# Experts of a mixture-of-experts stage taken in blocks of 64 tokens, not 32, and a new order of the half-width products

## The chip, the cores and the metric

The kernel runs on one core of one Trainium2 chip. The metric is device time in microseconds (us) of one execution; the smaller is the better.

## What is computed

Three transformer blocks one after the other on a sequence of 256 tokens, model width 1024, all in 32-bit floats. The change touches the mixture of experts of the first block and some projections of all three. The mixture, cut to what matters:

```python
logits = h @ w_router + b_router            # 256 tokens, 32 experts
top_v, top_i = lax.top_k(logits, 4)         # each token goes to 4 experts
gates = softmax(top_v)
# for each expert e and the tokens xb that chose it:
u = xb @ w_mlp1[e] + b_mlp1[e]              # 1024 -> 2048
x_glu = minimum(u[..., ::2], 7.0)
x_lin = clip(u[..., 1::2], -7.0, 7.0)
a = x_glu * sigmoid(1.702 * x_glu) * (x_lin + 1)
y = a @ w_mlp2[e] + b_mlp2[e]               # 1024 -> 1024
# out[token] += gate * y
```

The weights of an expert are 12 MB, so that the 32 experts read 384 MB.

## The kernel before

**The expert loop.** An expert's tokens are taken in passes of at most `C1` = 32; every expert has at least one pass. VectorE computes on the chip how many passes each expert needs and writes a list to `work`; all engines loop over that list. In one pass TensorE does the following, in the order of `expert_pass`: the first half of the up product of pass n (`up(n, 0, e)`), the transposes of the hidden activations of pass n-1 (`turn_hidden`), the gather of the tokens of pass n+1 by a product with a 0/1 matrix (`gather`), the down product of pass n-1 (`down`), the transposes of the gathered tokens (`turn_tokens`), the second half of the up product with the bias row (`up(n, 1, e)`), the product that adds the outputs of pass n-1 to the four sum banks (`scatter`), and the transposes of the way back (`back`). ScalarE copies each result out of PSUM, VectorE does the gated activation.

**Narrow products.** With 32 tokens as the stationary operand a matmul uses 32 of TensorE's 128 columns. The up product therefore puts four blocks of 512 output columns side by side, each in a strip of 32 columns (`C1 * c`), all in bank 0 of PSUM; gather and down do the same. Each product of 32-bit floats stands in the trace as two matmul instructions, so that the up product has 64 of them in a pass, and the down product 32.

**The slabs.** An expert's weights lie in six slabs of 2 MB, each with one place in SBUF and no second buffer. Slabs 0 to 3 hold `w_mlp1`: 0, 1, 2 in `ring`, 3 in `MOD`. Slabs 4 and 5 hold `w_mlp2`: 4 in `HTY`, 5 in `scr`. Slabs 0 to 3 are loaded by SP's queue, 4 and 5 by POOL's. The load of the next expert into a place is issued when the last pass of the expert before has used it: for 0, 1 and 2 after each one's last matmul, for 3 at the end of the up product, for 4 at the middle of `down` (`down_begun`) and for 5 at its end (`down`):

```python
pool.wait_ge(m1["down_begun"], through)
expert_slab(e, 4)
pool.wait_ge(m1["down"], through)
expert_slab(e, 5)
```

**The half-width products.** `features` computes a projection with features on the partitions. Where an argument is a pair (`twice`), the 64 columns of the weights are multiplied twice, into partitions 0 to 63 and 64 to 127 of the bank. The loop (line 702) goes over the eight parts of the contraction, and in it over the two halves; the matmul is on line 704. All other products of this kind go through `mm_k` (line 669).

Of the kernel before, what the change touches and what calls it, by code (L numbers as in the profile page):

```python
# [29 lines left out]
FLOOR = -1.0e20  # L30
C1 = 32
STRIPS1 = 4
PASSES = E1 + TOP1 * S // C1
# [109 lines left out]
def build(nc, I, out, rel_scratch):  # L143
    first, end, first_slab, release = product_plan()
    landed = landed_plan()
    with ExitStack() as ctx:
# [46 lines left out]
        def carve(base, *shape):  # L193
# [42 lines left out]
            "counted", "listed", "masked", "pick", "pick_back", "gather", "slots_read", "turn_tokens", "gather_read", "back", "back_read",  # L236
            "up", "up_read", "glu", "sig", "hidden", "turn", "turn_read", "gates_turned", "gates_read", "down_begun", "down", "down_read",
            "scatter", "sum", "sum_read", "step")}
        m1_slab_used = [sem(f"m1_slab_used{j}") for j in range(3)]
# [35 lines left out]
        b1row = scr[:, 0:BANK]  # L275
        XG, XS, GPT = carve(512, KT, C1), carve(768, S), carve(1024, S)
        PICK, PICKG = carve(1280, NT, C1), carve(1344, NT, STRIPS1, C1)
        glu, lin1, sig, aS = carve(1600, S), carve(1856, S), carve(2112, S), carve(2368, S)
        aT, YS = carve(2624, 2, P), carve(2880, BANK)
        GT, EPLACE, MASK = carve(5248, NT, E1), carve(5312, NT, E1), carve(5376, NT, E1)  # L280
        MASKED, LX = carve(5440, 3 * E1), carve(5536, NT, E1)
        LOGITS1, CHOSEN1, TOPL = carve(5600, NT, 4 + E1), carve(5672, NT, 4 + E1), carve(5744, NT, 8)
        rcur, gcur = carve(5760, NT), carve(5762, NT)
        EPASS, ESTEPS, EMORE = carve(5764, E1), carve(5796, S // C1), carve(3392, E1, S // C1)
        OFFSET1, START1, PASSED1 = carve(3648, PASSES + 2), carve(3714, PASSES + 2), carve(7084, PASSES + 2, E1)
        WORK = carve(3780, END1)
        gatesT = scr[0:E1, 5804:6060]
        b2row = scr[0:E1, 6060:7084]

# [257 lines left out]
        def _(pool):  # L547
# [77 lines left out]
            with pool.Fori(1, E1) as e:  # L625
                through = pool.value_load(work[0:1, bass.ds(e + (THROUGH - 1), 1)], min_val=1, max_val=PASSES)
                pool.wait_ge(m1["down_begun"], through)
                expert_slab(e, 4)
                pool.wait_ge(m1["down"], through)
                expert_slab(e, 5)  # L630

# [18 lines left out]
        def _(pe):  # L650
# [45 lines left out]
            def features(cols_of, rhs=HT, nk=KT, m=P):  # L696

                b = bank()
                for i, c in enumerate(cols_of):
                    if isinstance(c, tuple):  # L700

                        for k in range(nk):
                            for half in range(2):
                                mm = pe.matmul(b[64 * half:64 * half + 64, S * i:S * (i + 1)], c[half](k), rhs[:, k, :],  # L704
                                               start=k == 0, stop=k == nk - 1)
                    else:
                        mm = mm_k(b[0:m, S * i:S * (i + 1)], c, lambda k: rhs[:, k, :], nk)
                close(mm)
# [240 lines left out]
            def gather(n):  # L949

                pe.wait_ge(m1["pick"], n + 1)
                if not (isinstance(n, int) and n == 0):
                    pe.wait_ge(m1["gather_read"], n)
                for a in range(NT):
                    for q in range(STRIPS1):
                        mm = pe.matmul(ps[C1 * q:C1 * (q + 1), 3, 0:S], PICK[:, a, :], H[:, a, S * q:S * (q + 1)],  # L956
                                       start=a == 0, stop=a == NT - 1)
                mm.then_inc(m1["gather"], 1)

            def turn_tokens(n):  # L960

                pe.wait_ge(m1["slots_read"], n + 1)
                for i in range(2):
                    mm = pe.transpose(ps[:, 3, P * i:P * (i + 1)], XS[:, i:S:2], ident[:, :])
                mm.then_inc(m1["turn_tokens"], 1)
# [9 lines left out]
            def up(n, b, e):  # L975
# [3 lines left out]
                for j in (2 * b, 2 * b + 1):  # L979
                    if j == 3:  # L980
                        pe.wait_ge(m1_row_landed, 16 * e + 16)
                    pe.wait_ge(m1_landed[j], 16 * e + 16)
                    for i in range(2):
                        for c in range(STRIPS1):
                            mm = pe.matmul(ps[C1 * c:C1 * (c + 1), 0, :], XG[:, 2 * j + i, :],  # L985
                                           m1_slabs[j][:, i, BANK * c:BANK * (c + 1)], start=j + i == 0, stop=False)
                    if j < 3:
                        mm.then_inc(m1_slab_used[j], 1)
                if b == 1:
                    for c in range(STRIPS1):  # L990
                        mm = pe.matmul(ps[C1 * c:C1 * (c + 1), 0, :], ones[32 * c:32 * c + 1, 0:C1], b1row[32 * c:32 * c + 1, :],  # L991
                                       start=False, stop=True)
                    mm.then_inc(m1["up"], 1)

            def turn_hidden(n):

                pe.wait_ge(m1["hidden"], n + 1)
                pe.wait_ge(m1["back_read"], n + 1)
                for i in range(2):
                    mm = pe.transpose(ps[:, 2, P * i:P * (i + 1)], aS[:, i:S:2], ident[:, :])  # L1000
                mm.then_inc(m1["turn"], 1)

            def down(n, e):

                pe.wait_ge(m1["turn_read"], n + 1)
                for j in (4, 5):
                    pe.wait_ge(m1_landed[j], 16 * e + 16)
                    for i in range(2):
                        for t in range(2):
                            c = 2 * (j - 4) + t  # L1010
                            for half in range(2):
                                r = 2 * C1 * half + C1 * t
                                mm = pe.matmul(ps[r:r + C1, 1, :], aT[:, i, C1 * c:C1 * (c + 1)],  # L1013
                                               m1_slabs[j][:, 2 * t + i, BANK * half:BANK * (half + 1)],
                                               start=j + i == 4, stop=j + i == 6)
                    mm.then_inc(m1["down_begun" if j == 4 else "down"], 1)

            def scatter(n, last=False):

                pe.wait_ge(m1["down_read"], n + 1)  # L1020
                for a in range(NT):
                    for half in range(2):
                        r = slice(2 * C1 * half, 2 * C1 * (half + 1))
                        mm = pe.matmul(sum_bank(a, half), GPT[r, P * a:P * (a + 1)], YS[r, :], start=False, stop=last,  # L1024
                                       skip_group_check=True)
# [5 lines left out]
            def expert_pass(n, e, e_before):  # L1031

                pe.wait_ge(m1["gather_read"], n + 1)
                up(n, 0, e)
                turn_hidden(n - 1)
                gather(n + 1)
                down(n - 1, e_before)
                turn_tokens(n + 1)
                up(n, 1, e)
# [16 lines left out]
            with pe.Fori(1, n_passes) as n:  # L1056
                expert_pass(n, expert_of(n), expert_of(n - 1))
            turn_hidden(n_passes - 1)
            down(n_passes - 1, expert_of(n_passes - 1))
# [286 lines left out]
        def _(act):  # L1346
# [168 lines left out]
            def slots(n):  # L1515
                act.wait_ge(m1["gather"], n + 1)
                act.activation(XS, ps[:, 3, 0:S], ACT.Copy).then_inc(m1["slots_read"], 1)

            def gathered(n):

                if not (isinstance(n, int) and n == 0):
                    act.wait_ge(m1["up"], n)
                act.wait_ge(m1["turn_tokens"], n + 1)
                act.activation(XG.rearrange("p (q i) c -> p i q c", i=2), ps[:, 3, 0:S].rearrange("p (i q c) -> p i q c", i=2, q=STRIPS1),
                               ACT.Copy).then_inc(m1["gather_read"], 1)
# [8 lines left out]

            def turned_hidden(n):
                act.wait_ge(m1["turn"], n + 1)
                act.activation(aT, two(ps[:, 2, :], P), ACT.Copy).then_inc(m1["turn_read"], 1)

            def outputs(n):

                act.wait_ge(m1["scatter"], n + 1)
                act.wait_ge(m1["down"], n + 1)
                act.activation(YS, ps[:, 1, :], ACT.Copy).then_inc(m1["down_read"], 1)  # L1543

            def expert_pass(n):
                turned_hidden(n - 1)
                slots(n + 1)
                outputs(n - 1)
                gathered(n + 1)
# [13 lines left out]
            with act.Fori(1, n_passes) as n:  # L1563
                expert_pass(n)
            turned_hidden(n_passes - 1)
            outputs(n_passes - 1)
# [152 lines left out]
        def _(dve):  # L1719
# [353 lines left out]
            def pick_back(n):  # L2073

                shape = [P, NT, STRIPS1, C1]
                tell(dve.tensor_tensor(PICKG[:, :, :, :], PICK.unsqueeze(2).to_broadcast(shape),
# [37 lines left out]
            def activation(n, astep):  # L2114

                dve.wait_ge(m1["up"], n + 1)
                tell(dve.tensor_scalar(glu, ps[:, 0, 0:BANK:2], 7.0, None, ALU.min), m1["glu"], n + 1)  # L2117
                tell(dve.tensor_scalar(lin1, ps[:, 0, 1:BANK:2], 7.0, -7.0, ALU.min, ALU.max), m1["up_read"], n + 1)
                dve.wait_ge(m1["sig"], n + 1)
# [313 lines left out]
```

## Time and profile before

| | |
|---|---|
| median of 3 runs | 2653.49 us (2651.34 to 2654.19) |
| the profiled execution | 2654.19 us |
| its span in the trace | 2652.4 us |
| busy: TensorE matmuls, VectorE, ScalarE | 2120.5, 500.4, 392.1 us |
| the expert loop of the first block in the trace | 329.19 to 1384.91 us |
| the chain that ended last | PE 61%, DMA 27%, DVE 6%, ACT 3% |

The profiled execution is longer than its span by 1.8 us, which lie around the instructions. PE is TensorE, DVE VectorE, ACT ScalarE, POOL GpSimd, SP the engine that only issues transfers. Busy time says little here by itself: a matmul's time in the trace runs from its start to its modelled end, and neighbours overlap. The distance from one start to the next is what a step costs.

### The profile page before, as it was taken

How to read it: one execution, taken by the hardware profiler on the slowest of the kernel's cores; microseconds unless marked ns; L12 is line 12 of the kernel's file. 1: busy time of each engine (PE TensorE's matmuls, PEld its weight loads, DVE VectorE, ACT ScalarE, POOL GpSimd, SP SyncE). 2: the span in 40 equal slices, each digit the busy share in tenths (PEclk: the TensorE clock that was granted, in tenths of full speed). 3: DMA queues.
4: the chain of work that ended last, by engine and by line, in shares of the span. 5: the costliest groups of instructions: out<-in, count | busy, mean ns of one | idle time of the engine just before them, and what ended most of it. 6: DMA issues, size and time to landing. Idle time of an engine off the chain costs nothing.

```text
span 2652.4 us, 34466 instructions
## 1 busy us (share of the span) xinstructions
PE 2120.5 (80%) x14230; PEld 1185.3 (45%) x14231; DVE 500.4 (19%) x1153; ACT 392.1 (15%) x864; POOL 87.4 (3%) x130
## 2 busy tenths in 40 slices
PE   4976769567767966979779886899969898977785
PEld 3856422112212211322227766689955546453443
DVE  1044421001101100111120375200041302230002
ACT  1142101001101100111111333100001113110011
POOL 4000000000000000000000000000000000000000
PEclk9995779779888987989899995999979999978898
DMA  9460589999999699997952581346424243079964
GB/s 304 121 244 13 208 364 396 426 425 386 384 425 383 284 426 426 373 399 300 384 199 106 197 291 53 127 159 158 136 103 143 104 134 127 32 299 393 391 261 191
DMA packets 170904, 681.33 MB, mean 257 GB/s; under 512 B 15906, under 2 KB 57123, under 8 KB 125520
## 3 DMA queue, kind: packets, MB, share of 16 engines
q1 hardware_dynamic: 149488, 535.79, 52.0%
q0 software_dynamic: 21328, 144.45, 14.1%
q8 instruction: 58, 0.95, 0.1%
q14 instruction: 14, 0.11, 0.0%
q10 hardware_dynamic: 16, 0.02, 0.0%
HBM read 679.17 MB, written 1.06 MB: 256 GB/s over the span
## 4 chain that ended last, share of the span: by engine, by line
PE 61%; DMA 27%; DVE 6%; ACT 3%; issue 2%; SPq 1%; POOLq 0%; DVEq 0%; POOL 0%; ACTq 0%
PE ps L669 29%; DMA scr<-in_w_mlp 20%; PE ps L985 7%; PE ps L1013 6%; DMA MOD<-in_w 5%; PE ps L1284 3%; PE ps L1024 2%; PE ps L746 2%; DMA ring<-in_w_ada 1%; PE ps L704 1%; PE ps L848 1%; PE ps L756 1%; PE ps L956 1%; DVE stat L1749 1%; PE ps L991 1%
## 5 line engine op out<-in xcount | busy, mean ns | idle before, releaser
L985 PE MATMUL ps<-ring,scr 128*32 128x512 f32 x2208 | 289.2, 656 | 65.7 <-DMA ring<-in_w_mlp 63.4
L669 PE MATMUL ps<-ring,HTY 128*128 128x512 f32 (+5 forms) x960 | 331.0, 506 | 3.7 <-ACT HTY L1365 3.7
L669 PE MATMUL ps<-HTY,ring 128*128 128x256 f32 x1136 | 253.1, 386 | 2.4 <-ACT HTY L1365 2.4
L1013 PE MATMUL ps<-scr 128*32 128x512 f32 x736 | 119.9, 782 | 166.9 <-DMA scr<-in_w_mlp 166.9
L669 PEld LDWEIGHTS ps<-ring,HTY 128*128 128x128 f32 x960 | 176.5, 192 | 155.1 <-issue 138.8
L669 PEld LDWEIGHTS ps<-HTY,ring 128*128 128x128 f32 x1136 | 218.2, 193 | 36.1 <-ACT HTY L1365 3.7
L2117 DVE TENSOR_SCALAR scr<-ps 128x256 f32<-128x256 f32 x46 | 19.6, 425 | 822.6 <-PE ps L991 822.5
L985 PEld LDWEIGHTS ps<-ring,scr 128*32 128x32 f32 x2208 | 64.3, 117 | 215.6 <-issue 131.0
L1365 ACT ACTIVATE scr<-ps 128x512 f32<-128x512 f32 (+8 forms) x120 | 59.1, 494 | 527.4 <-PE ps L669 416.5
L1013 PEld LDWEIGHTS ps<-scr 128*32 128x32 f32 x736 | 25.1, 129 | 241.8 <-DMA scr<-in_w_mlp 185.8
L669 PE MATMUL ps<-ring,scr 128*128 128x128 f32 (+1 forms) x1040 | 121.6, 280 | 1.4 <-DVE scr L2221 1.4
L669 PEld LDWEIGHTS ps<-ring,scr 128*128 128x128 f32 x1040 | 117.5, 192 | 5.2 <-issue 3.3
L1284 PE MATMUL ps<-ring,scr 128*32 128x512 f32 x432 | 76.7, 693 | 50.9 <-DMA MOD<-in_w 50.3
L1013 PE MATMUL ps<-HTY,scr 128*32 128x512 f32 x736 | 89.1, 602 | 6.7 <-DMA HTY<-in_w_mlp 6.2
L1024 PE MATMUL ps<-scr 64*128 64x512 f32 x368 | 91.4, 615 | 0.8 <-ACT scr L1543 0.8
L985 PE MATMUL ps<-MOD,scr 128*32 128x512 f32 x736 | 87.3, 592 | 1.0 <-DMA MOD<-in_w_mlp 1.0
L1543 ACT ACTIVATE scr<-ps 128x512 f32<-128x512 f32 x46 | 27.5, 597 | 354.8 <-PE ps L1013 354.8
L669 PE MATMUL ps<-scr,H 128*128 128x128 f32 x320 | 77.9, 405 | 1.6 <-DVE scr L2335 1.6
L746 PE MATMUL ps<-ring,cols 128*32 128x128 f32 x1536 | 51.3, 290 | 34.3 <-DMA ring<-in_w_ada 34.3
L669 PEld LDWEIGHTS ps<-scr,H 128*128 128x128 f32 x320 | 77.0, 335 | 1.7 <-DVE scr L2335 1.7
L1284 PE MATMUL ps<-MOD,scr 128*32 128x512 f32 x144 | 76.6, 693 | 0.0
L1284 PEld LDWEIGHTS ps<-ring,scr 128*32 128x32 f32 x432 | 21.1, 126 | 105.0 <-issue 104.1
(416 smaller groups left out, 2039.5 us busy)
## 6 DMA issues: line engine op xcount, KB each, us to landing
ring<-in_w_mlp SPq DMA_DIRECT2D x96, 2048.0 KB, 14.3
scr<-in_w_mlp POOLq DMA_DIRECT2D x32, 2048.0 KB, 23.9
MOD<-in_w_mlp SPq DMA_DIRECT2D x32, 2048.0 KB, 19.0
HTY<-in_w_mlp POOLq DMA_DIRECT2D x32, 2048.0 KB, 18.9
ring<-in_w_ada SPq DMA_DIRECT2D x24, 2048.0 KB, 9.1
ring<-in_w SPq DMA_DIRECT2D x48, 1024.0 KB, 10.4
ring<-in_w_in SPq DMA_DIRECT2D x21, 2048.0 KB, 7.8
ring<-in_w_ff SPq DMA_DIRECT2D x16, 2048.0 KB, 8.8
```

What stands on the lines that cost most here:

```text
L669: mm = pe.matmul(o, lhs(k), rhs(k), start=begin and k == 0, stop=end and k == nk - 1)
L704: mm = pe.matmul(b[64 * half:64 * half + 64, S * i:S * (i + 1)], c[half](k), rhs[:, k, :], start=k == 0, stop=k == nk - 1)
L746: pe.matmul(b[32 * t:32 * (t + 1), 0:P], csil[:, j, k:k + 1].to_broadcast([P, 32]), w[:, k, P * t:P * (t + 1)], start=k == 0, stop=False)
L756: mm = pe.matmul(b[:, P * t:P * (t + 1)], ident[:, 32 * t:32 * t + 1].to_broadcast([P, P]), ada_quarters[j], start=True, stop=True)
L848: mm = pe.matmul(o, KDb[:, i % 2, pair, P * tile:P * (tile + 1)], QD[:, pair, i, :, :], start=True, stop=True)
L956: mm = pe.matmul(ps[C1 * q:C1 * (q + 1), 3, 0:S], PICK[:, a, :], H[:, a, S * q:S * (q + 1)], start=a == 0, stop=a == NT - 1)
L985: mm = pe.matmul(ps[C1 * c:C1 * (c + 1), 0, :], XG[:, 2 * j + i, :], m1_slabs[j][:, i, BANK * c:BANK * (c + 1)], start=j + i == 0, stop=False)
L1013: mm = pe.matmul(ps[r:r + C1, 1, :], aT[:, i, C1 * c:C1 * (c + 1)], m1_slabs[j][:, 2 * t + i, BANK * half:BANK * (half + 1)], start=j + i ...
L1024: mm = pe.matmul(sum_bank(a, half), GPT[r, P * a:P * (a + 1)], YS[r, :], start=False, stop=last, skip_group_check=True)
L1284: mm = pe.matmul(ps[32 * t:32 * (t + 1), 0, :].rearrange("p (x f) -> p x f", x=2), XG3[:, k, C3 * t:C3 * (t + 1)], m3_slabs[t][:, :, k, :] ...
L1365: act.activation(dst, src, func, **kw).then_inc(product_free, 1)
L1543: act.activation(YS, ps[:, 1, :], ACT.Copy).then_inc(m1["down_read"], 1)
```

## The change

1. `C1` becomes 64. A pass takes up to 64 tokens, and each narrow matmul is 64 columns wide, so that two lie side by side and not four. The up product goes into banks 0 and 1, the gather fills a whole bank, `turn_tokens` has four transposes, the hidden activations are twice as wide and are transposed in two steps through the same half of bank 2 (`turn_hidden(n, 0)`, `turn_hidden(n, 1)`, with a copy by ScalarE between them), and `down` accumulates all four parts of the contraction in bank 2.
2. In the pass, the order is up 0, turn 0, gather, turn 1, `turn_tokens`, down, up 1, scatter, back.
3. POOL issues slabs 4 and 5 together, after `down`.
4. In `features` the halves are the outer loop, the parts of the contraction the inner one.

```diff
-C1 = 32
-STRIPS1 = 4
+C1 = 64
...
-                pool.wait_ge(m1["down_begun"], through)
-                expert_slab(e, 4)
                 pool.wait_ge(m1["down"], through)
-                expert_slab(e, 5)
+                for j in (4, 5):
+                    expert_slab(e, j)
...
-                        for k in range(nk):
-                            for half in range(2):
-                                mm = pe.matmul(b[64 * half:64 * half + 64, S * i:S * (i + 1)], c[half](k), rhs[:, k, :],
-                                               start=k == 0, stop=k == nk - 1)
+                        for half in range(2):
+                            mm = mm_k(b[64 * half:64 * half + 64, S * i:S * (i + 1)], c[half], lambda k: rhs[:, k, :], nk)
...
-                    for q in range(STRIPS1):
-                        mm = pe.matmul(ps[C1 * q:C1 * (q + 1), 3, 0:S], PICK[:, a, :], H[:, a, S * q:S * (q + 1)],
+                    for half in range(2):
+                        mm = pe.matmul(ps[C1 * half:C1 * (half + 1), 3, :], PICK[:, a, :], H[:, a, BANK * half:BANK * (half + 1)],
                                        start=a == 0, stop=a == NT - 1)
...
-                        for c in range(STRIPS1):
-                            mm = pe.matmul(ps[C1 * c:C1 * (c + 1), 0, :], XG[:, 2 * j + i, :],
+                        for c in range(4):
+                            mm = pe.matmul(ps[C1 * (c % 2):C1 * (c % 2 + 1), c // 2, :], XG[:, 2 * j + i, :],
                                            m1_slabs[j][:, i, BANK * c:BANK * (c + 1)], start=j + i == 0, stop=False)
...
-            def turn_hidden(n):
+            def turn_hidden(n, b):
 
                 pe.wait_ge(m1["hidden"], n + 1)
-                pe.wait_ge(m1["back_read"], n + 1)
+                if b == 0:
+                    pe.wait_ge(m1["back_read"], n + 1)
+                else:
+                    pe.wait_ge(m1_turn_read[0], n + 1)
                 for i in range(2):
-                    mm = pe.transpose(ps[:, 2, P * i:P * (i + 1)], aS[:, i:S:2], ident[:, :])
-                mm.then_inc(m1["turn"], 1)
+                    mm = pe.transpose(ps[:, 2, P * i:P * (i + 1)], aS[:, b, i:S:2], ident[:, :])
+                mm.then_inc(m1_turn[b], 1)
 
             def down(n, e):
-
-                pe.wait_ge(m1["turn_read"], n + 1)
+                pe.wait_ge(m1_turn_read[1], n + 1)
                 for j in (4, 5):
                     pe.wait_ge(m1_landed[j], 16 * e + 16)
-                    for i in range(2):
-                        for t in range(2):
-                            c = 2 * (j - 4) + t
-                            for half in range(2):
-                                r = 2 * C1 * half + C1 * t
-                                mm = pe.matmul(ps[r:r + C1, 1, :], aT[:, i, C1 * c:C1 * (c + 1)],
-                                               m1_slabs[j][:, 2 * t + i, BANK * half:BANK * (half + 1)],
-                                               start=j + i == 4, stop=j + i == 6)
-                    mm.then_inc(m1["down_begun" if j == 4 else "down"], 1)
+                    for t in range(2):
+                        for i in range(2):
+                            for s in range(2):
+                                mm = pe.matmul(ps[C1 * s:C1 * (s + 1), 2, :], aT[:, 2 * (j - 4) + i, C1 * t:C1 * (t + 1)],
+                                               m1_slabs[j][:, 2 * t + i, BANK * s:BANK * (s + 1)],
+                                               start=j + t + i == 4, stop=j + t + i == 7)
+                mm.then_inc(m1["down"], 1)
...
                 up(n, 0, e)
-                turn_hidden(n - 1)
+                turn_hidden(n - 1, 0)
                 gather(n + 1)
+                turn_hidden(n - 1, 1)
+                turn_tokens(n + 1)
                 down(n - 1, e_before)
-                turn_tokens(n + 1)
                 up(n, 1, e)
```

ScalarE's and VectorE's instructions in the loop follow the new shapes: their copies and activations read 512 columns where they read 256, and ScalarE has one copy more in a pass.

## Rows read from the trace of the kernel before

**Rows 1.** Timeline of TensorE, one pass that waits for nothing: start, time.

```profile
430.92 3.64 PE L985 MATMUL ps<-ring,scr 128*32 128x512 f32 x32
434.49 0.51 PE L1000 MATMUL ps<-ident,scr 128*128 128x128 f32 x2
434.93 1.07 PE L956 MATMUL ps<-H,scr 128*32 128x256 f32 x16
435.82 1.90 PE L1013 MATMUL ps<-HTY,scr 128*32 128x512 f32 x16
...
439.37 0.50 PE L964 MATMUL ps<-ident,scr 128*128 128x128 f32 x2
...
443.37 1.06 PE L991 MATMUL ps<-scr,ones 1*32 1x512 f32 x8
444.36 1.99 PE L1024 MATMUL ps<-scr 64*128 64x512 f32 x8
...
446.65 0.64 PE L985 MATMUL ps<-ring,scr 128*32 128x512 f32 x4
```

**Rows 2.** Timeline of TensorE, where passes wait for slabs: idle time before, and releaser.

```profile
530.64 1.92 PE L985 MATMUL ps<-ring,scr 128*32 128x512 f32 x16 [2.59 <-DMA ring<-in_w_mlp]
...
971.14 3.64 PE L1013 MATMUL ps<-scr 128*32 128x512 f32 x16 [10.55 <-DMA scr<-in_w_mlp]
...
999.85 3.64 PE L1013 MATMUL ps<-scr 128*32 128x512 f32 x16 [8.93 <-DMA scr<-in_w_mlp]
```

**Rows 3.** Windows, four experts of one pass: busy (x), then clock, DMA share, GB/s.

```profile
484.20:603.90 119.70, 77.81 (x540) 20.58 (x544) 11.00 (x32) 10.21 (x24) 5.64 (x8) 0.80 1.01 426
```

**Rows 4.** The chain that ended last, its first and last piece of line 704.

```profile
79.78 7.06 PE ps L704 x64
...
2208.79 5.33 PE ps L704 x48
```

**Rows 5.** The page's costliest groups: VectorE's first step on an up product.

```profile
L2117 DVE TENSOR_SCALAR scr<-ps 128x256 f32<-128x256 f32 x46 | 19.6, 425 | 822.6 <-PE ps L991 822.5
```

**Rows 6.** Issues of SP's queue in the loop: start, time, line, tile.

```profile
834.53 0.33 SPq L450 DMA_DIRECT2D MOD<-in_w_mlp  x1
...
900.23 0.33 SPq L450 DMA_DIRECT2D MOD<-in_w_mlp  x1
```

**Rows 7.** TensorE's groups by form: busy, mean ns of one, idle before.

```profile
L669 PE MATMUL ps<-HTY,ring 128*128 128x256 f32 x1120 | 249.5, 386 | 2.4 <-ACT HTY L1365 2.4
...
L704 PE MATMUL ps<-HTY,ring 128*64 128x256 f32 x256 | 28.5, 381 | 0.0
...
L704 PE MATMUL ps<-scr,ring 128*64 128x256 f32 x96 | 10.8, 381 | 0.0
...
L669 PE MATMUL ps<-HTY,ring 128*16 128x256 f32 x16 | 3.6, 380 | 0.0
```

**Rows 8.** DMA queues in that window: packets, MB, share of 16 engines.

```profile
q1 hardware_dynamic: 2321, 33.34, 65.7%
q0 software_dynamic: 2294, 17.61, 35.2%
```

**Rows 9.** Timeline of POOL there: an issue of slab 5.

```profile
975.47 0.70 POOL L612 DMA_DIRECT2D scr<-in_w_mlp  x1 [13.36 <-PE ps L1013]
```

**Rows 10.** The page's transfers: how many, KB each, median us from issue to landing.

```profile
ring<-in_w_in SPq DMA_DIRECT2D x21, 2048.0 KB, 7.8
```

**Rows 11.** Timeline of TensorE, the loop's start.

```profile
329.19 8.10 PE L985 MATMUL ps<-ring,scr 128*32 128x512 f32 x48 [0.47 <-ACT scr L1524]
...
338.93 1.06 PE L991 MATMUL ps<-scr,ones 1*32 1x512 f32 x8
...
355.16 5.35 PE L985 MATMUL ps<-ring,scr 128*32 128x512 f32 x32 [1.78 <-issue]
```

**Rows 12.** Timeline of all engines, the loop's end.

```profile
1373.52 1.06 PE L991 MATMUL ps<-scr,ones 1*32 1x512 f32 x8
...
1384.91 1.94 ACT L1569 ACTIVATE HTY<-ps 128x1024 f32<-128x1024 f32 x2 [2.09 <-PE ps L1024]
```

More of the change, by code:

```diff
@@ L236, in build @@
             "counted", "listed", "masked", "pick", "pick_back", "gather", "slots_read", "turn_tokens", "gather_read", "back", "back_read",
-            "up", "up_read", "glu", "sig", "hidden", "turn", "turn_read", "gates_turned", "gates_read", "down_begun", "down", "down_read",
-            "scatter", "sum", "sum_read", "step")}
+            "up", "up_read", "glu", "sig", "hidden", "gates_turned", "gates_read", "down", "down_read", "scatter", "sum", "sum_read", "step")}
+        m1_turn, m1_turn_read = ([sem(f"m1_{n}{b}") for b in range(2)] for n in ("turn", "turn_read"))
         m1_slab_used = [sem(f"m1_slab_used{j}") for j in range(3)]
@@ L275, in build @@
         b1row = scr[:, 0:BANK]
[L276 to L279, printed above, removed]
+        XG, XS, GPT = carve(512, KT, C1), carve(1024, BANK), carve(1536, S)
+        PICK, PICKG = carve(1792, NT, C1), carve(1920, NT, 2, C1)
+        glu, lin1, sig, aS = carve(2176, 2, 256), carve(2688, 2, 256), carve(3200, 2, 256), carve(3712, 2, 256)
+        aT, YS = carve(4224, 4, P), carve(4736, BANK)
         GT, EPLACE, MASK = carve(5248, NT, E1), carve(5312, NT, E1), carve(5376, NT, E1)
@@ L283, in build @@
         rcur, gcur = carve(5760, NT), carve(5762, NT)
[L284 to L288, printed above, removed]
+        EPASS, ESTEPS, EMORE = carve(5764, E1), carve(5796, S // C1), carve(7264, E1, S // C1)
+        OFFSET1, START1, PASSED1 = carve(5800, PASSES + 2), carve(5850, PASSES + 2), carve(7392, PASSES + 2, E1)
+        WORK = carve(5900, END1)
+        gatesT = scr[0:E1, 5984:6240]
+        b2row = scr[0:E1, 6240:7264]
         m1_slabs = [shaped(ring[:, j, :], (2, 2 * F1)) for j in range(3)] + [
@@ L962, in turn_tokens @@
                 pe.wait_ge(m1["slots_read"], n + 1)
-                for i in range(2):
-                    mm = pe.transpose(ps[:, 3, P * i:P * (i + 1)], XS[:, i:S:2], ident[:, :])
+                for jj in range(2):
+                    for i in range(2):
+                        k = 2 * jj + i
+                        mm = pe.transpose(ps[:, 3, P * k:P * (k + 1)], XS[:, S * jj + i:S * (jj + 1):2], ident[:, :])
                 mm.then_inc(m1["turn_tokens"], 1)
@@ L989, in up @@
                 if b == 1:
-                    for c in range(STRIPS1):
-                        mm = pe.matmul(ps[C1 * c:C1 * (c + 1), 0, :], ones[32 * c:32 * c + 1, 0:C1], b1row[32 * c:32 * c + 1, :],
-                                       start=False, stop=True)
+                    for c in range(4):
+                        mm = pe.matmul(ps[C1 * (c % 2):C1 * (c % 2 + 1), c // 2, :], ones[32 * c:32 * c + 1, 0:C1],
+                                       b1row[32 * c:32 * c + 1, :], start=False, stop=True)
@@ L1003, in down @@
             def down(n, e):
-                pe.wait_ge(m1["turn_read"], n + 1)
+                pe.wait_ge(m1_turn_read[1], n + 1)
                 for j in (4, 5):
                     pe.wait_ge(m1_landed[j], 16 * e + 16)
-                    for i in range(2):
-                        for t in range(2):
-                            c = 2 * (j - 4) + t
-                            for half in range(2):
-                                r = 2 * C1 * half + C1 * t
-                                mm = pe.matmul(ps[r:r + C1, 1, :], aT[:, i, C1 * c:C1 * (c + 1)],
-                                               m1_slabs[j][:, 2 * t + i, BANK * half:BANK * (half + 1)],
-                                               start=j + i == 4, stop=j + i == 6)
-                    mm.then_inc(m1["down_begun" if j == 4 else "down"], 1)
+                    for t in range(2):
+                        for i in range(2):
+                            for s in range(2):
+                                mm = pe.matmul(ps[C1 * s:C1 * (s + 1), 2, :], aT[:, 2 * (j - 4) + i, C1 * t:C1 * (t + 1)],
+                                               m1_slabs[j][:, 2 * t + i, BANK * s:BANK * (s + 1)],
+                                               start=j + t + i == 4, stop=j + t + i == 7)
@@ L1022, in scatter @@
                     for half in range(2):
-                        r = slice(2 * C1 * half, 2 * C1 * (half + 1))
+                        r = slice(C1 * half, C1 * (half + 1))
                         mm = pe.matmul(sum_bank(a, half), GPT[r, P * a:P * (a + 1)], YS[r, :], start=False, stop=last,
@@ L1057, in _ @@
                 expert_pass(n, expert_of(n), expert_of(n - 1))
-            turn_hidden(n_passes - 1)
+            turn_hidden(n_passes - 1, 0)
+            turn_hidden(n_passes - 1, 1)
             down(n_passes - 1, expert_of(n_passes - 1))
@@ L1516, in slots @@
                 act.wait_ge(m1["gather"], n + 1)
-                act.activation(XS, ps[:, 3, 0:S], ACT.Copy).then_inc(m1["slots_read"], 1)
+                act.activation(XS, ps[:, 3, :], ACT.Copy).then_inc(m1["slots_read"], 1)
             def gathered(n):
@@ L1523, in gathered @@
                 act.wait_ge(m1["turn_tokens"], n + 1)
-                act.activation(XG.rearrange("p (q i) c -> p i q c", i=2), ps[:, 3, 0:S].rearrange("p (i q c) -> p i q c", i=2, q=STRIPS1),
+                act.activation(XG.rearrange("p (h k) c -> p k h c", h=2), ps[:, 3, :].rearrange("p (k h c) -> p k h c", k=4, h=2),
                                ACT.Copy).then_inc(m1["gather_read"], 1)
@@ L1533, in gate, with turned_hidden @@
                 act.activation(sig, glu, ACT.Sigmoid, scale=1.702).then_inc(m1["sig"], 1)
-            def turned_hidden(n):
-                act.wait_ge(m1["turn"], n + 1)
-                act.activation(aT, two(ps[:, 2, :], P), ACT.Copy).then_inc(m1["turn_read"], 1)
+            def turned_hidden(n, b):
+                act.wait_ge(m1_turn[b], n + 1)
+                act.activation(aT[:, 2 * b:2 * b + 2, :], two(ps[:, 2, :], P), ACT.Copy).then_inc(m1_turn_read[b], 1)
             def outputs(n):
@@ L1542, in outputs @@
                 act.wait_ge(m1["down"], n + 1)
-                act.activation(YS, ps[:, 1, :], ACT.Copy).then_inc(m1["down_read"], 1)
+                act.activation(YS, ps[:, 2, :], ACT.Copy).then_inc(m1["down_read"], 1)
             def expert_pass(n):
-                turned_hidden(n - 1)
+                turned_hidden(n - 1, 0)
                 slots(n + 1)
+                turned_hidden(n - 1, 1)
                 outputs(n - 1)
@@ L1564, in _ @@
                 expert_pass(n)
-            turned_hidden(n_passes - 1)
+            turned_hidden(n_passes - 1, 0)
+            turned_hidden(n_passes - 1, 1)
             outputs(n_passes - 1)
@@ L2073, in pick_back @@
             def pick_back(n):
-                shape = [P, NT, STRIPS1, C1]
+                shape = [P, NT, 2, C1]
                 tell(dve.tensor_tensor(PICKG[:, :, :, :], PICK.unsqueeze(2).to_broadcast(shape),
@@ L2116, in activation @@
                 dve.wait_ge(m1["up"], n + 1)
-                tell(dve.tensor_scalar(glu, ps[:, 0, 0:BANK:2], 7.0, None, ALU.min), m1["glu"], n + 1)
-                tell(dve.tensor_scalar(lin1, ps[:, 0, 1:BANK:2], 7.0, -7.0, ALU.min, ALU.max), m1["up_read"], n + 1)
+                tell(dve.tensor_scalar(glu, ps[:, 0:2, 0:BANK:2], 7.0, None, ALU.min), m1["glu"], n + 1)
+                tell(dve.tensor_scalar(lin1, ps[:, 0:2, 1:BANK:2], 7.0, -7.0, ALU.min, ALU.max), m1["up_read"], n + 1)
                 dve.wait_ge(m1["sig"], n + 1)
```

## Prediction

> **What bounds the kernel now.** I read the chain of waits first. Its pieces in the expert loop are of two kinds: transfers of expert weights, and TensorE's own work. The timeline of TensorE shows that they take turns. An expert that needs several passes gives passes without a wait: the next begins 446.65 - 430.92 = 15.73 us later [rows 1]. An expert of one pass waits for its slabs, for slab 5 above all, and the next pass comes 28.7 us later [rows 2]. There the DMA engines are full: 24 slabs in 119.7 us, 426 GB/s at a share of 1.01 [rows 3], so 4.99 us a slab and 29.9 us an expert. Outside the loop the chain holds long pieces of TensorE work, and all six pieces of line 704 are in it [rows 4].
>
> **How many passes go.** VectorE's first step on an up product ran 46 times [rows 5], so there are 46 passes. An expert of k passes shows as a gap in SP's issues: slab 3 was issued at 834.53 and next at 900.23 [rows 6], 65.7 us later, one waiting pass and two of 15.73. Read in this way, three experts (17, 27 and 31, counted from 0) have three passes, eight have two, 21 have one. Three passes of 32 are 65 to 96 tokens, which are two passes of 64; all others fit in one. So 35 passes stay and 11 go. The bytes stay.
>
> **What a pass costs then.** Four matmuls of 32 columns side by side take as long as one: 32 of 512 columns took 434.49 - 430.92 = 3.57 us [rows 1], which is 8 groups of 0.4275 and 0.15 for the switch of shape. The trace has 64-column matmuls too: 256 of 256 columns on line 704 in 28.5 us, 0.111 each, while full-width ones took 0.223 [rows 7]; two go side by side. So each narrow product needs twice the groups. By steps, from [rows 1]:
> - up, each half: 16 groups, 6.84 + 0.15 = 7.0 (was 3.57).
> - down: 7.0 (was 439.37 - 435.82 = 3.55).
> - gather: 4 groups of 512 columns, 1.8 (was 0.89).
> - transposes of hidden: 0.43 twice. The second waits for a copy, which the gather hides.
> - transposes of tokens: four, 0.8, and about 0.35 before them, since the copy of the gathered bank (some 0.6 to 0.8 us with its start, an estimate from VectorE's 0.425 for half the columns [rows 5]) is covered by 0.43 of transposes only. Behind this wait stands `down`.
> - bias row: four row strips, two column strips, 0.99 if all four run together as now, 1.85 if only two. I take 0.99.
> - scatter and back: unchanged, 446.65 - 444.36 = 2.3. They cover VectorE's two reads of the wider up result (some 0.7 each, twice the columns of [rows 5]) and ScalarE's copy of the next tokens; uncovered, these would cost 1.4.
>
> Sum: 14.0 + 7.0 + 1.8 + 0.86 + 1.15 + 0.99 + 2.3 = 28.1 us, 29.0 with the slower bias. A pass costs 12.4 us more of TensorE's time than one of 32, and comes just under the 29.9 us that an expert's weights take.
>
> **What an expert of one pass costs.** It can't be under 29.9, the slabs, for long. Above that, POOL's queue decides. With both queues at work POOL moved 17.61 MB while SP moved 33.34, in packets equal in number [rows 8], so SP has a slab in 7.5 us and POOL one in 15.0 (16 and 8 of them in 119.7). Slab 5's landings are 999.85 - 971.14 = 28.7 us apart [rows 2], two POOL slabs, 14.2 each when SP pauses, and 975.47 - 971.14 = 4.3 us of it go by while slab 5 is used and issued [rows 2, 9]; slab 4's load fills that gap today. After the change POOL's queue has nothing while slab 5 is used, and both are issued at the end of `down`. Count from there: POOL's data start at 3.4 us (7.8 from issue to landing of a slab [rows 10], less 5.0 of data, plus 0.7 to issue), run alone until SP's slab 2, freed at 3.4, begins at 6.3, and then share. Slab 4 has 2.9/5.0 of itself by then and lands at 12.3 to 12.6, slab 5 at 26.5 to 27.6 (14.2 or 15.0 each), its use takes 3.5: a cycle of 30.0 to 31.1. Were POOL always to share, it would be 3.4 + 30.0 + 3.5 = 37. I take 30.5, the middle. The wait is then 2.4 us a pass; after one of 2.59 us the next 16 matmuls took 1.92 us, after one of 8.93 they took 3.64, at the lower clock [rows 2].
>
> The Trainium skill ("DMA: Bandwidth & Descriptors", Queues, rings and completion order) says each engine goes round the queues packet by packet, so POOL's share would stay a third in pairs too. The equal packet counts agree; by it the even share of a rival below is out.
>
> **The loop's sum.** The first up product took 338.93 - 329.19 = 9.74 [rows 11]; 16 groups more make 16.6, to 345.8. From there to pass 1, 16.2 now [rows 11], 16.5 then. Pass 1 to its bias row: 7.0 + 3.8 + 7.0 + 7.0, to 387.1. Then 33 passes: 28 wait for slab 5 (30.5 each, 854.0), 5 don't, those after the slabs of an expert with two passes (28.1, 140.5). To 1381.6. From the last bias row to the end it was 1384.91 - 1373.52 = 11.4 [rows 12]; `down` adds 3.5, the second turn 1.1: 16.0. End 1397.6, against 1384.9: **+12.7 us.** The 11 passes that go are 11 x 15.73 = 173 us; the 35 left cost TensorE 35 x 12.4 = 434 more, and only what fills the waits of now is free.
>
> **The half-width products.** Halves outside means that neighbours use the same 64 columns. The nearest row is 16 matmuls of 16 columns, one after the other on the same columns: 3.6 us, 0.225 each, as long as full width [rows 7]. So 352 matmuls cost 0.223 and not 0.111: 352 x 0.1115 = **+39.2 us**. All of it is on the chain (six pieces, 38.9 us in sum, [rows 4]), between TensorE work that waits for nothing, idle 0.0 before them [rows 7]; the weights of the next slabs are loaded when TensorE frees a place, so they come later as well. If neighbours overlapped still, it would be 0.
>
> VectorE's tables of the pass list shrink (from 66 rows of 32 to 50); TensorE doesn't wait for them: 0.
>
> Total: 2654.2 + 12.7 + 39.2 = **2706 us**, 1.9% over its own execution; the median of the runs is 0.7 us lower, which the range swallows.
>
> **Rivals.**
> - *TensorE becomes the only bound of the loop* (faster). If slabs came in time always, 33 passes at 28.1 are 927 us, 67 less: 2639. Place: the wait at slab 5. It breaks even with the 39.2 where the 28 passes average 30.5 - 51.9/28 = 28.6 us. Against it: 29.9 of data. For it: the passes of now are 28.7 apart [rows 2]. Chance 0.05.
> - *POOL's pair is late* (much slower): the sharing cycle of 37 in half of the passes, or longer waits that bring the lower clock: 33 on the mean, 28 x 2.5 = 70 more, 2776. Chance 0.12.
> - *The order of halves costs nothing*, TensorE overlapping them otherwise: 2667. Against it [rows 7], chance 0.04.
> - *POOL gets an even share in its pair*: 29.9 a pass, 2689; inside my range, and its chance is in the forecast's.
>
> **How the numbers follow.** Forecast 0.79 (2675 to 2740), rivals 0.05, 0.12, 0.04. A measurement here tells 0.2%, 5 us, from no change. Faster takes the first rival; same is its edge with that of the third: 0.06, 0.04, slower 0.90. The low end, 2668, is the free halves, or 29.1 a pass; the high end, 2755, is 32.3 a pass. Outside lie the first rival and most of the second.
>
> **What would show it.** 35 steps on line 2117's successor, each of 0.69 us; the up half 7.0 us long; passes 30 to 31 us apart with a wait of 2 to 3 us before slab 5's matmuls; DMA share near 1 in them; 28.1 without a wait; line 704 gone, its 352 matmuls in pieces twice as long, 0.22 apart. Wrong if narrow matmuls of two banks don't pair, if POOL's share changes, or if the pieces of the halves stay as short.

## The result, and the profile after

The changed kernel took 2681.84 us (median of 4 runs, 2680.85 to 2687.45) beside 2653.84 us for the kernel before on the same chip: 1.011 times as long, 95% interval 1.0094 to 1.0129. The forecast was 2706 us, range 2668 to 2755.

Its span is 2680.8 us, 28.4 more. The first up product starts at 333.62 instead of 329.19, the loop ends at 1396.33 instead of 1384.91 [rows 11, 12]. So 4.4 us arise before the loop, 7.0 in it (1062.7 for 1055.7), and 17.0 behind it. The two ends of the loop in the timeline of the changed kernel:

```profile
333.62 12.02 PE L983 MATMUL ps<-ring,scr 128*64 128x512 f32 x48 [0.69 <-ACT scr L1524]
...
1396.33 1.94 ACT L1571 ACTIVATE HTY<-ps 128x1024 f32<-128x1024 f32 x2 [2.09 <-PE ps L1022]
```

Such parts scatter by some 4 us from one execution to another: in two of the experiments below, whose kernels are equal up to there, the first up product starts at 331.70 (e1) and 327.60 (e3).

The page of the changed kernel, from its costliest groups (busy, mean ns of one, idle before), with the successor of [rows 5]:

```profile
L2119 DVE TENSOR_SCALAR scr<-ps 128x512 f32<-128x512 f32 x35 | 24.2, 692 | 842.9 <-PE ps L989 842.9
```

There are 35 passes, and VectorE's wider step takes 0.692 us. Next the timeline of TensorE in the changed kernel, a pass that waits for no slab, to be laid beside [rows 1]:

```profile
886.63 0.51 PE L1001 MATMUL ps<-ident,scr 128*128 128x128 f32 x2
887.07 1.94 PE L952 MATMUL ps<-H,scr 128*64 128x512 f32 x8
888.94 0.50 PE L1001 MATMUL ps<-ident,scr 128*128 128x128 f32 x2
889.70 0.75 PE L962 MATMUL ps<-ident,scr 128*128 128x128 f32 x4 [0.26 <-ACT scr L1517]
890.38 3.65 PE L1011 MATMUL ps<-HTY,scr 128*64 128x512 f32 x16
893.87 3.60 PE L1011 MATMUL ps<-scr 128*64 128x512 f32 x16
897.30 3.60 PE L983 MATMUL ps<-ring,scr 128*64 128x512 f32 x16
...
904.27 1.09 PE L989 MATMUL ps<-scr,ones 1*64 1x512 f32 x8
905.28 1.99 PE L1022 MATMUL ps<-scr 64*128 64x512 f32 x8
907.20 0.44 PE L969 MATMUL ps<-ident,scr 128*128 128x128 f32 x2
```

Read from start to start: gather 1.87, transposes of tokens 0.68 after a wait of 0.26 for ScalarE's copy, down 897.30 - 890.38 = 6.92, half of up 904.27 - 897.30 = 6.97, bias row 1.01 (all four of its matmuls side by side), scatter 1.92. The whole pass is 27.96 us.

The same view where a pass waits:

```profile
499.76 5.35 PE L1011 MATMUL ps<-scr 128*64 128x512 f32 x16 [2.57 <-DMA scr<-in_w_mlp]
...
511.91 1.09 PE L989 MATMUL ps<-scr,ones 1*64 1x512 f32 x8
...
530.54 3.65 PE L1011 MATMUL ps<-scr 128*64 128x512 f32 x16 [0.91 <-DMA scr<-in_w_mlp]
...
540.99 1.09 PE L989 MATMUL ps<-scr,ones 1*64 1x512 f32 x8
```

The only slab that passes wait for is slab 5. Among experts of one pass, most passes alternate: one waits 0.7 to 1.0 us and is about 29 long, the next waits 2.0 to 4.0 us and is 32 to 35 long. The difference is more than the wait, because behind the wait of 2.57 us 16 matmuls took 5.35 us instead of 3.65: the granted clock fell to its lower level (1.2 GHz) for a while. The windows over one pass of each kind, and over the use of slab 5 in each, show it in the third column from the end (the clock; DMA share and GB/s follow):

```profile
479.50:511.90 32.40, 29.57 (x132) 9.75 (x130) 3.88 (x8) 3.46 (x7) 1.40 (x2) 0.95 0.95 393
511.90:541.00 29.10, 27.93 (x133) 9.40 (x132) 3.88 (x8) 3.46 (x7) 1.40 (x2) 1.00 1.01 428
...
499.76:504.94 5.18, 5.18 (x16) 1.59 (x18) 0.00 (x0) 0.00 (x0) 0.00 (x0) 0.67 0.98 418
504.94:508.40 3.46, 3.46 (x20) 1.17 (x18) 0.00 (x0) 0.60 (x1) 1.40 (x2) 1.00 0.45 118
530.54:534.03 3.49, 3.49 (x17) 1.21 (x19) 0.00 (x0) 0.00 (x0) 0.00 (x0) 1.00 1.01 432
534.03:537.50 3.47, 3.47 (x20) 1.19 (x18) 0.00 (x0) 0.60 (x1) 1.40 (x2) 1.00 0.96 408
```

In the second and fourth of these four windows, right behind the use of slab 5, the new pair has just been issued. After the longer wait the DMA engines were half idle there (0.45): SP's queue had run out as well (0.5% of the engines' time from 505.4 to 507). After the shorter one SP's queue alone kept them busy (0.96).

The page's groups of TensorE by form, for the half-width products, the successors of two of [rows 7]:

```profile
L667 PE MATMUL ps<-HTY,ring 128*64 128x256 f32 x256 | 46.4, 382 | 0.0
...
L667 PE MATMUL ps<-scr,ring 128*64 128x256 f32 x96 | 11.8, 381 | 0.0
```

The same 352 matmuls take 58.2 us where they took 39.3: 18.9 more, of which 4.0 lie before the loop (64 matmuls from 79.67 to 90.73, 11.1 us where they took 7.1 [rows 4]).

### The profile page after: what moved, and what is told of

It reads as the page before. It is cut to its first block, busy times and chain, and to the rows that moved or that the text cites. A ratio compares the mean times of both kernels' runs of the same rounds, so it can differ in the third digit from the quotient of the medians.

```text
span 2680.8 us, 30691 instructions
## 1 busy us (share of the span) xinstructions
PE 2333.5 (87%) x12610; PEld 1300.5 (49%) x12611; DVE 507.6 (19%) x1065; ACT 395.9 (15%) x833; POOL 87.0 (3%) x130
## 4 chain that ended last, share of the span: by engine, by line
PE 58%; DMA 29%; DVE 6%; ACT 3%; issue 2%; SPq 1%; POOLq 0%; POOL 0%; DVEq 0%; ACTq 0%
PE ps L667 31%; DMA scr<-in_w_mlp 23%; PE ps L1011 7%; PE ps L983 5%; DMA MOD<-in_w 5%; PE ps L1284 3%; PE ps L742 2%; DMA ring<-in_w_ada 1%; PE ps L844 1%; PE ps L752 1%; PE ps L952 1%; DVE stat L1751 1%; PE ps L678 1%; PE ps L802 1%; PE ps L1022 1%
## 5 line engine op out<-in xcount | busy, mean ns | idle before, releaser
L983 PE MATMUL ps<-ring,scr 128*64 128x512 f32 x1680 | 376.9, 598 | 2.7 <-issue 2.0
L667 PE MATMUL ps<-HTY,ring 128*128 128x256 f32 (+2 forms) x1392 | 300.7, 386 | 2.4 <-ACT HTY L1365 2.4
L667 PEld LDWEIGHTS ps<-HTY,ring 128*128 128x128 f32 (+2 forms) x1392 | 249.3, 183 | 51.9 <-ACT HTY L1365 3.7
L983 PEld LDWEIGHTS ps<-ring,scr 128*64 128x64 f32 x1680 | 118.3, 138 | 231.5 <-issue 230.5
L1011 PE MATMUL ps<-scr 128*64 128x512 f32 x560 | 145.5, 668 | 43.5 <-DMA scr<-in_w_mlp 43.5
L1011 PE MATMUL ps<-HTY,scr 128*64 128x512 f32 x560 | 127.9, 598 | 0.6 <-ACT scr L1537 0.6
L983 PE MATMUL ps<-MOD,scr 128*64 128x512 f32 x560 | 126.1, 592 | 0.0
L1284 PE MATMUL ps<-ring,scr 128*32 128x512 f32 x432 | 78.2, 704 | 51.9 <-DMA MOD<-in_w 51.2
L1284 PE MATMUL ps<-MOD,scr 128*32 128x512 f32 x144 | 78.0, 704 | 0.0
L952 PE MATMUL ps<-H,scr 128*64 128x512 f32 x288 | 73.1, 630 | 1.5 <-DVE scr L2066 1.5
```

What stands on the lines that cost most here:

```text
L667: mm = pe.matmul(o, lhs(k), rhs(k), start=begin and k == 0, stop=end and k == nk - 1)
L952: mm = pe.matmul(ps[C1 * half:C1 * (half + 1), 3, :], PICK[:, a, :], H[:, a, BANK * half:BANK * (half + 1)], start=a == 0, stop=a == NT - 1)
L983: mm = pe.matmul(ps[C1 * (c % 2):C1 * (c % 2 + 1), c // 2, :], XG[:, 2 * j + i, :], m1_slabs[j][:, i, BANK * c:BANK * (c + 1)], start=j + ...
L1011: mm = pe.matmul(ps[C1 * s:C1 * (s + 1), 2, :], aT[:, 2 * (j - 4) + i, C1 * t:C1 * (t + 1)], m1_slabs[j][:, 2 * t + i, BANK * s:BANK * (s ...
L1284: mm = pe.matmul(ps[32 * t:32 * (t + 1), 0, :].rearrange("p (x f) -> p x f", x=2), XG3[:, k, C3 * t:C3 * (t + 1)], m3_slabs[t][:, :, k, :] ...
```

## The experiments

All but three were timed in turns with the kernel before; their ratios have it as 1.

**Halves interleaved again, the rest as changed** (`e1_halves_inside`).

```diff
-                        for half in range(2):
-                            mm = mm_k(b[64 * half:64 * half + 64, ...], c[half], lambda k: rhs[:, k, :], nk)
+                        for k in range(nk):
+                            for half in range(2):
+                                mm = pe.matmul(b[64 * half:64 * half + 64, ...], c[half](k), rhs[:, k, :], ...)
```

> The changed kernel with the halves of the half-width products interleaved again, as before the change. Theory: the order of the halves costs 18.9 us (the 352 matmuls took 58.2 us of the changed kernel's trace against 39.3 before), so this runs in 2681.8 - 18.9 = 2663 us. Rival, the forecast's price: it gives back 39.2, 2643. Second rival: the cost of the halves in the trace is hidden elsewhere, 2682.

Measured: 2669.1 us (2662.4 to 2671.6), ratio 1.0058 (1.0043 to 1.0072). Its 352 matmuls are back at 28.5 and 10.8 us. By the medians the new order costs 12.7 us, by the ratios 14; the runs scatter by some 5. The forecast's price of 39 is out, and so is no cost at all.

**The new order of halves alone, in the kernel before** (`e2_halves_outside_alone`): the diff's part 4 and nothing else.

> The kernel before with the new order of the halves alone. Theory: + 18.9 us, 2672.7, with the same 58.2 us for the 352 matmuls. Rival (neighbours on the same columns never overlap): + 39.2, 2693.

Measured: 2675.3 us (2666.4 to 2678.7), ratio 1.0079 (1.0062 to 1.0095), 16 to 25 us; 46.4 and 11.8 us for the 352 matmuls. The theory's 18.9 lies inside, the 39 of the forecast outside.

**Slab 4 issued at the middle of down again, halves interleaved, blocks of 64** (`e3_slab4_at_half`).

```diff
-                pool.wait_ge(m1["down"], through)
-                for j in (4, 5):
-                    expert_slab(e, j)
+                pool.wait_ge(m1["down_begun"], through)
+                expert_slab(e, 4)
+                pool.wait_ge(m1["down"], through)
+                expert_slab(e, 5)
...
-                mm.then_inc(m1["down"], 1)
+                    mm.then_inc(m1["down_begun" if j == 4 else "down"], 1)
```

> As e1_halves_inside, and slab 4 is issued at the middle of the down product, slab 5 at its end, as before the change. Theory (POOL's queue stands empty while slab 5 is used, and that is why passes that wait for it are 30.7 us apart on the mean): they come down to the 29.9 us that the six slabs take, 28 x 0.8 = 22 us less than e1, about 2641. Rival (the 30.7 is the slabs' own time, or another wait takes its place): the same as e1, 2663.

Measured: 2641.5 us (2636.1 to 2646.0), ratio 0.9958 (0.9942 to 0.9974); timed once more beside e9 (`e10_split_again`) 2642.3, ratio 0.9959. This is 28 us less than e1. The chain of waits names the same releaser in both; first the changed kernel, then this one (total, times, longest):

```profile
PE ps L1011 <- DMA scr<-in_w_mlp: 43.5, 25, 4.0
```

```profile
PE ps L1014 <- DMA scr<-in_w_mlp: 24.5, 10, 3.6
```

From 25 waits to 10 (e1, whose diff to this kernel is the issue alone, has 25 of together 44.5 us). The 33 passes behind the first take 958.9 us, for 985.8 in e1. The windows of this kernel over the use of slab 5 behind a wait of 2.77 us, and the stretch behind it, show what changed: the clock falls as before, but the DMA engines stay full, since slab 4 is already under way.

```profile
1046.24:1051.42 5.18, 5.18 (x17) 1.60 (x18) 0.00 (x0) 0.00 (x0) 0.00 (x0) 0.67 0.99 421
1051.42:1054.90 3.48, 3.48 (x20) 1.20 (x18) 0.00 (x0) 0.60 (x1) 0.70 (x1) 1.00 0.99 414
```

**Slabs 4 and 5 issued together, in the kernel before** (`e4_joint_issue_alone`): the diff's part 3 and nothing else.

> The kernel before with slabs 4 and 5 issued together at the end of the down product, nothing else. Theory: the waits for slab 5 grow, since two slabs of POOL's queue (26.5 to 27.6 us from the issue at the end of down to landing) and then its use (1.9 to 3.6 us) follow each other with nothing beside them: passes that wait go from 28.7 to about 29.5 to 30, + 15 us, 2669. Rival: the queue's total work is the same and DMA is full, no change.

Measured: 2690.0 us (2684.2 to 2691.4), ratio 1.0136 (1.0119 to 1.0153): 38 us, more than double the 15 expected. The timelines of POOL and of TensorE in this kernel:

```profile
968.44 0.71 POOL L612 DMA_DIRECT2D HTY<-in_w_mlp  x1 [36.79 <-PE ps L1012]
969.14 0.70 POOL L612 DMA_DIRECT2D scr<-in_w_mlp  x1
```

```profile
964.01 3.64 PE L1012 MATMUL ps<-scr 128*32 128x512 f32 x16 [12.69 <-DMA scr<-in_w_mlp]
...
980.44 1.92 PE L1012 MATMUL ps<-HTY,scr 128*32 128x512 f32 x16 [0.28 <-DMA HTY<-in_w_mlp]
994.58 3.64 PE L1012 MATMUL ps<-scr 128*32 128x512 f32 x16 [12.22 <-DMA scr<-in_w_mlp]
```

Slab 5 comes 26.1 us after the pair's issue, and 30.6 us after its predecessor; before it was 28.7 [rows 2]. The mechanism and the cycle (30 to 31.1) are as forecast. The expectation was short: it moved passes of 28.7 to 29.5 or 30 us; the seven full cycles went to 29.5 to 30.9, and of the nine first waiting passes behind an expert of several passes (or behind the start of the loop) five, 35 to 37 us long before, went to 37 to 38.6. By the trace the passes hold 29.7 of the 36 us of its span; the rest lies outside of the loop and isn't traced. The chain of waits in this kernel:

```profile
PE ps L1012 <- DMA scr<-in_w_mlp: 211.3, 24, 12.7
...
PE ps L1012 <- DMA HTY<-in_w_mlp: 22.9, 15, 8.0
```

Waits for slab 5 rose from 166.9 us to 211.3, those for slab 4 from 6.2 to 22.9, while those for slabs 0 to 2 fell from 63.4 to 38.3.

**Halves taking turns after runs of 8 matmuls** (`e5_runs_of_eight`): the loop over the halves stands between a loop over blocks of four parts and the loop inside a block. It ran once, in 2663.2 us; the reading rests on its trace.

> The changed kernel; the halves take turns after four parts of the contraction, that is after runs of 8 matmul instructions, where the changed kernel has runs of 16 and the kernel before runs of 2. Theory: TensorE starts up to about five matmuls of the other columns beside the end of a run, so a run of 16 takes 2.65 us (12.3 starts of 0.216) and a run of 8 would take 4.3 starts, 0.93 us: the 352 half-width matmuls are busy for about 41 us, near the 39.3 of runs of 2. Rival (runs overlap only where neighbours alternate): about 70 us, since 7 of 8 would stand alone.

Measured, in the groups of TensorE by form:

```profile
L703 PE MATMUL ps<-HTY,ring 128*64 128x256 f32 x256 | 33.5, 385 | 0.0
...
L703 PE MATMUL ps<-scr,ring 128*64 128x256 f32 x96 | 11.8, 381 | 0.0
```

The 96 had runs of 6 in the changed kernel and have runs of 6 at most here (11.8 in both). It is 45.3 in all, nearer the theory's 41 than the rival's 70. So runs of 2, 8 and 16 cost 0.111, 0.131 and 0.181 us a matmul. The expectation's "about five" is nearer four (see the windows further down).

**The loops without most of the weights** (`e6_new_without_slabs`, `e7_old_without_slabs`): from expert 1 on, the transfers bring a part of each slab only, so that the products use old weights. Each ran once.

```diff
+                n = 2 * F1 if isinstance(e, int) else 128
-                sp.dma_start(m1_slabs[j], ... [2 * P * j:2 * P * (j + 1), :] ...
+                sp.dma_start(m1_slabs[j][:, :, 0:n], ... [:, :, 0:n]) ...
```

> The changed kernel in which the slabs of experts 1 to 31 load only a sixteenth of their data (slabs 0 to 3) or less (an eighth for slabs 4 and 5, in half of their rows), so that the products use old weights; waits and matmuls stay. Theory: the waits for slabs are all that passes lose, so every pass after the first takes 27.96 us, the 33 of them 923 instead of 989.6, and the run 2681.8 - 67 = 2615 us. Rival (TensorE loses time in the loop otherwise): more than 2640.

Measured: 2624.4 us. The 33 passes take 922.7 us, each 27.96, as expected; the 9 us over the 2615 lie outside of them, 4.8 of it before the first bias row. The timeline of TensorE, two neighbouring bias rows:

```profile
620.40 1.09 PE L993 MATMUL ps<-scr,ones 1*64 1x512 f32 x8
648.36 1.09 PE L993 MATMUL ps<-scr,ones 1*64 1x512 f32 x8
```

> The same cut of the slabs in the kernel before. Theory: passes of 15.73 us throughout, 45 x 15.73 = 708 us instead of 1034.6, so 2653 - 327 = 2326 us, that is, with no weights to wait for, blocks of 64 would be some 290 us slower than blocks of 32. Rival (the 46 passes bound the loop of the kernel before, as their removal supposes): little faster than 2653.

Measured: 2349.0 us, and in the same view of this kernel:

```profile
603.95 1.06 PE L995 MATMUL ps<-scr,ones 1*32 1x512 f32 x8
619.67 1.06 PE L995 MATMUL ps<-scr,ones 1*32 1x512 f32 x8
```

Every pass behind the first takes 15.72 us (the first 32.1, which is most of the 23 us over the theory). With the slabs out of the way the changed kernel is 275 us slower than the kernel before, whose 46 passes hide in the waits for weights; 231 of it lie in the passes behind the first (922.7 for 691.7), 18.9 in the order of the halves.

**Slab 4 early, the new order of halves kept** (`e8_split_with_new_halves`): e3's diff on the changed kernel.

> The changed kernel with slab 4 issued at the middle of the down product and the new order of the halves kept. Theory (the parts add up): e3_slab4_at_half plus 19, about 2660; against the changed kernel 22 to 28 us less. Rival: the gain of e3 came from the halves, so it stays at 2682.

Measured: 2656.2 us (2645.3 to 2660.2), ratio 1.0014 (1.0002 to 1.0026): 26 us less than the changed kernel and 15 more than e3. The parts add up within the scatter, which is wide here.

**Slabs 4 and 5 in halves of 1 MB** (`e9_half_slabs`), with e3's kernel beside it.

```diff
+                for h in range(4):
+                    pool.wait_ge(m1_half_used[h], through)
+                    expert_half(e, 4 + h // 2, h % 2)
...
                     for t in range(2):
+                        h = 2 * (j - 4) + t
+                        pe.wait_ge(m1_half_landed[h], 16 * e + 16)
...
+                        mm.then_inc(m1_half_used[h], 1)
```

> Halves interleaved as before the change, C1 = 64, and slabs 4 and 5 loaded in halves of 1 MB with semaphores of their own, each issued when its own half is used. Theory (POOL's queue must never stand empty, and a pass that waits should wait for 1 MB only): the waits of e3_slab4_at_half, 24.5 us and some 17 us more at the lower clock behind them, shrink by half, 2641 - 20 = 2621 to 2630. Rival (the six slabs' 29.5 to 29.9 us are the bound already): as e3, 2641.

> The kernel of e3_slab4_at_half once more, beside e9 on the same chip, to have their difference: 2641, 0.4% under the kernel before.

Measured: e9 2633.8 us (2630.6 to 2641.8), ratio 0.9929 (0.9913 to 0.9946); e10 2642.3 us, 0.9959 (0.9943 to 0.9976). The halved slabs gain 8 us, under the 11 to 20 expected:

```profile
PE ps L1020 <- DMA scr<-in_w_mlp: 22.2, 8, 3.0
```

8 waits of together 22.2 us are left, so the waits did not halve; in the traces the 33 passes take 956.5 us, for 961.7 in e10. A reason, not tested: where experts of one pass follow each other, TensorE needs 27.96 us for each and the data 29.9, so some waiting has to stay. It is the fastest version here that loads all weights, 0.7% under the kernel before.

## Why the prediction was right, and where its sizes were off

**Passes, right.** 46 became 35.

**A pass, right.** 28.1 us forecast, 27.96 measured (e6 shows it bare). Column strips of 64 pair up as the 64-column products before did. The tokens' transposes with their wait were 0.94, not 1.15, gather 1.87, not 1.8.

**The wait for slab 5: the place and the cycle right, what fills it in part wrong.** 28 passes at 30.5 and 5 at 28.1 were forecast, 994.5 us; there were 25 with a mean of 30.64 and 8 at 27.96, 989.6 us. Slab 5 landed every 30.7 us on the mean between 499.76 and 714.66, seven times, whatever the clock did. That the joint issue, with nothing in POOL's queue while slab 5 is used, costs this is shown from both sides: it costs 38 us in the kernel before (e4), and its removal gives 28 after (e1 to e3), with the DMA engines full in a window where they were half idle.

The count of the cycle assumed that POOL's pair starts alone, with SP's queue empty. That was so in every second pass only (DMA share 0.45 behind the long use of slab 5, 0.96 behind the short one). The end of `down` to slab 5's landing was then 25.6 and 27.4 us by turns, where 26.5 to 27.6 was forecast, and the longer of the two follows the shorter use, so that the sum stays the same.

What the forecast had wrong here is "after one of 2.59 us the next 16 matmuls took 1.92": a wait of that length can bring the lower clock too. It expected 28 waits of 2.4 us, 67 in all, and nothing for the clock. Of the 989.6 - 33 x 27.96 = 67 us that passes lose, only 43.5 are waits. 18 are the slower matmuls behind ten of them (16 took 5.2 to 6.6 us for 3.65), and the 5 that are left are 0.2 at each wait (29.1 = 27.96 + 0.91 + 0.2), where the matmuls before and behind it can't overlap as neighbours do. That 67 came out both times is no luck as far as the cycle sets it; that the clock took only time that would have been waited for was not foreseen.

**The loop, +12.7 forecast, +7.0 measured.** First up product to its bias row 15.4 (16.6 forecast), from there to pass 1's bias row 41.6 (41.3), 33 passes 989.6 (994.5), end 16.1 (16.0): 1062.7 for 1068.4. The same loop took 3.8 us less behind its first pass in e1, so the difference of 5.7 is hardly more than scatter.

**The half-width products, mis-sized.** The step that failed is "neighbours use the same 64 columns ... 352 x 0.1115 = +39.2". It took the row of 16 columns, which has only one column strip, for the whole run. Measured: + 18.9 us in the trace, 13 to 23 in the timed pairs (e1, e2, and e8 against e3). A run's matmuls do stand alone, but its end overlaps with the beginning of the next run on the other half. So the case that the forecast priced at 0, neighbours that overlap still, holds for a few matmuls at each change of half. Windows over the first of these products in the changed kernel, the matmuls counted in the first bracket, in turn inside a run and at a change of half:

```profile
80.00:81.70 1.70, 1.70 (x10) 1.07 (x9) 0.00 (x0) 0.00 (x0) 0.00 (x0) 1.00 0.52 1
81.80:82.60 0.80, 0.80 (x9) 0.64 (x8) 0.00 (x0) 0.00 (x0) 0.00 (x0) 1.00 1.18 2
82.80:84.40 1.60, 1.60 (x10) 1.05 (x8) 0.00 (x0) 0.00 (x0) 0.00 (x0) 1.00 0.43 70
84.40:85.30 0.90, 0.90 (x10) 0.70 (x9) 0.00 (x0) 0.00 (x0) 0.00 (x0) 1.00 0.81 278
```

Ten matmuls touch 1.7 us inside a run, and nine 0.8 us at its end. Windows that grow in small steps give the starts: from 79.90 to 81.85 one every 0.217 us; at 81.85, and again at 84.50, two at once. From one change to the next are 2.65 us for 16 matmuls, where 16 at 0.217 would take 3.47: about four starts are saved at each change. That most or all of the cost is on the path, as forecast, is what e1 and e2 show: 13 to 23 us in the timed pairs for 18.9 in the trace.

**The sum.** 7.0 in the loop and 18.9 for the halves are 25.9 of the 28.4 us; the rest, 2.5 us, isn't traced to a cause and is within the scatter of runs. Both terms were forecast too large, the second by a factor of two, and the whole with them: 28 us for 52. The result lies inside the range, near its low end. Of the rivals none came. *TensorE the only bound* would have been passes of 27.96 throughout: 67 us less in the passes (e6), and the kernel before would have been beaten. Of *POOL's pair is late* the lower clock came, but not the longer cycle. *POOL gets an even share in its pair* is out: the DMA queues of the changed kernel from 512 to 522 us, with transfers of both under way throughout, show equal packets and a third of the bytes for POOL (q0), as forecast.

```profile
q1 hardware_dynamic: 190, 2.85, 66.6%
q0 software_dynamic: 193, 1.45, 34.3%
```

**Where the gain of 11 passes went.** By e3, blocks of 64 alone (with the new order in the pass) are worth 10 to 12 us and not the 173 that the passes cost TensorE, since the slabs' 29.9 us an expert bound the old loop (e7: without them the kernel before is 304 us shorter), and a pass of 27.96 us comes just under them (e6: the changed kernel is 57 us shorter). The change then gave this back, and more, with the issue of slab 4 (28 us) and the order of the halves (13 to 23).

## What to carry to other kernels

Fewer and fuller passes help a loop that waits for weights only by what they let the transfers do; read first whether the transfers are full, and then which queue is empty while its last buffer is used. Give back each buffer as soon as its own last reader is through: two buffers of one queue released together cost more here (28 us) than eleven passes less gained (11). Where matmuls are narrower than the array, let neighbours alternate between column strips, with the loop over the strips inside; the other order cost 13 to 23 us here.

## What the hardware showed that was not expected

- Matmuls of two column strips overlap over a limited look ahead. With runs of 2, 6, 8 and 16 matmuls on one half, each of 256 columns, one costs 0.111, 0.123, 0.131 and 0.181 us; alone 0.217. About four of the next run start beside the end of a run of 16, an estimate from 2.65 us between changes for 3.47.
- Waits of nearly the same length were followed by either clock. In the changed kernel ten waits of 2.01 to 3.96 us were followed by slower matmuls (16 in 5.35 us behind 2.57), the 14 of up to 1.76 us were not, and neither was one of 2.58 us, nor in the kernel before one of 2.59 us [rows 2].

```profile
1313.84 3.65 PE L1011 MATMUL ps<-scr 128*64 128x512 f32 x16 [2.58 <-DMA scr<-in_w_mlp]
```
